# The attention phase of two layers, from four blocks one after the other to one stream of 80 slots

## The chip, the cores and the metric

The kernel is one program on one core of a Trainium2 chip. The metric is the time of one execution in microseconds on the device. The engines are TensorE (PE, with its weight loads as PEld), VectorE (DVE), ScalarE (ACT), GpSimd (POOL) and SyncE (SP, which only issues transfers here). They run in parallel, each through its own list of instructions in order, and wait for each other on semaphores.

## What is computed

An input of 512 positions by 1024 channels goes through two blocks of a network with three kinds of attention, and then through one block with dilated attention and a convolution. The change touches the attention of the first two layers, between the projections and the merging of the three branches:

```python
# 1: stick-breaking, 4 heads, weights from a cumulative sum over keys
w = exp(log_sigmoid(z) + tail);  o_a = w @ v
# 2: NSA, 8 heads in 2 groups, three parts, each with its gate
o_b = g0 * (softmax(q kc, compressed keys) @ vc) \
    + g1 * (softmax(q ks) @ vs) + g2 * (softmax(q kw) @ vw)
# 3: DSA, 4 heads over the 256 keys with the highest index score
score = sum_h(relu(iq_h @ ik) * iw_h)
o_c = softmax(q k[top 256]) @ v
merged = g_a * (o_a @ w_br_a) + g_b * (o_b @ w_br_b) + g_c * (o_c @ w_br_c)
```

All is float32. Where float32r is used, each factor is split in a high and a low part and three products are summed.

## The kernel before, in words

A layer is five phases: feed-forward, `mix1` (projections), `mix2` (attention), `mix3` (gates, branches, output), feed-forward. Between phases stands `fence`, at which all engines meet. The layers are one hardware loop of two rounds. The change is in `mix2`, whose four lists are `mix2_pe`, `mix2_act`, `mix2_dve` and `mix2_pool`, and in the order of the rows of one weight in the host's preparation.

`mix2` goes over four blocks `b` of 128 queries. Keys of block `b` are the first 128 (b + 1). A block has 20 jobs: batches 0 to 3 of four heads each are NSA (two for selected keys, two for the window), batch 4 is DSA. A job is: three score products (L893) into one of two banks; DVE adds the mask, turns the sign and takes the minimum (L1129); ACT takes the exponential and its sum `den` (L994) into `prob`. When a batch has its four jobs, DVE makes `coef`, one over the sum times the gate (L1112, L1117), ACT multiplies three heads of `prob` by it (L974) and POOL the fourth (L1035). PE then transposes the four heads for each key block (L905), ACT copies the result to `prob_t` (L1010), and PE multiplies it with the values (L915), 128 columns of values by 512 of weights, into the banks 4, 5 and 7. The columns of values are those of two groups, so half of each such result is not used. The compressed part is scaled in `cmp_p` and its product (L882) is summed in the same banks. At the end of a block ACT copies the used parts of the three banks to `o_t` (L1020).

The order is written by hand in slots. At slot `j` PE does the scores of job `j + 2`, then up to three `pieces` (transposes and value products of a batch that is complete), and then a step of `stick`, the stick-breaking attention of head `b`, whose products go to bank 6 (L818, L828, L830, L837) and whose exponentials and logarithm are at ACT's slots 7, 8 and 18. The slots run to 25 in each block. Before slot 0 of block `b` > 0 stand the eight index heads (L851, then ACT's relu L967 and DVE's sum L1078) and the compressed scores (L865, L1093 to L1106). For `b` > 0 DVE also picks the 256 highest index scores, eight in each of the jobs 0 to 15 (L1136, L1137), for the mask of batch 4.

At the start of `mix2`, ACT and DVE split the queries and keys into high and low parts, three tiles of 512 columns at a time (L979, L1083).

Of the kernel before, what the change touches and what calls it, by code (L numbers as in the profile page):

```python
# [7 lines left out]
P = 128  # L8
# [52 lines left out]
def program(nc, A, out, layers=L, dumps=()):  # L61
# [59 lines left out]
    relu, neg_s = val, sq  # L121
    index_s, picked, mask_k = ssq, val[0], val[1]
    prob = [part2.tensor(f"prob{i}", 4 * S) for i in range(2)]
    prob_t = [part2.tensor(f"prob_t{i}", S) for i in range(2)]
# [4 lines left out]
    kc_hi = idle.tensor("kc_hi", NC, F32R)  # L129
    assert idle.at <= w_hi_at + 8 * UNIT * 4  # L130
    cmp_s, cmp_t = (part2.tensor(n, 256) for n in ("cmp_s", "cmp_t"))
    cmp_p = cmp_s
    cmp_m = part2.tensor("cmp_m", 16)
    top8 = part2.tensor("top8", 8)
    neg_m = part2.tensor("neg_m", 80)
    den = part2.tensor("den", 80)
    coef = part2.tensor("coef", 80)
    zsq2 = relu
# [79 lines left out]
    for n in ("gains_in bias_tab_in bias_mm bias_out_a bias_out_v glu qk_out o_out conv job_parts mean centred c_norm c_val c_hi c_lo ya_out x_post y_norm "  # L218
              "sq_summed stat_sum stat_std stat_rs stat_diag rstd h_f32 h_hi h_lo "
              "dve_step x_val x_hi x_lo pad sb_out v_out t_out turned roped small_out hid cmp_mm cmp_turned mixer_in zn head_sum head_std gates vcb_zero "  # L220
              "job_red job_sc job_exp job_tr job_pv pt_out gate up gate_free rs_out hid_n hid_tr split_hi split_lo coef scaled_a scaled_p cmp_scaled sb_z sb_sp sb_c sb_w sb_o sb_d sb_zm sb_abs sb_e sb_ln idx_mm idx_relu idx_acc "
              "cmp_sc cmp_exp cmp_tr cmp_pt cmp_o cmp_sub merged_o o_hi o_lo o_tr sig branches part_sum m_val m_hi m_lo "
              "silu prod act_hi act_lo x_new sq zeroed ssq_add").split():
        s[n] = sem(n)
# [507 lines left out]
    def scores_q(tile_i, half, b):  # L732
        return heads_t[half, tile_i * S + b * P:tile_i * S + (b + 1) * P]

    JOBS, BATCHES = 20, 5
    ORDER = (0, 2, 1, 3)
    O_BANK = (4, 5, 4, 5, 7)  # L740

    def job(b, j):

        n, bt = (b + 1) * P, j // 4
        if bt < 4:
            c = ORDER[j % 4]
            half, t = slice(64 * (c // 2), 64 * (c // 2) + 64), 2 * (bt % 2) + c % 2
            key = (4 + bt // 2) * S
        else:
            c = j % 4  # L750
            half, t = slice(64 * (c % 2), 64 * (c % 2) + 64), 6 + c // 2
            key = 8 * S
        query = slice(t * S + b * P, t * S + (b + 1) * P)
        return bt, c, ((qk_hi[half, query], qk_lo[half, query]), (qk_hi[half, key:key + n], qk_lo[half, key:key + n]))

    def batch_values(bt, kb):

        if bt < 4:
            v0 = SB_H * HD + (bt // 2) * P
            return v_nat[:, kb * 512 + v0:kb * 512 + v0 + P]  # L760
        return small[:, kb * SMALL:kb * SMALL + P]

    def to_split():

        tiles = [slice(3 * i * S, 3 * (i + 1) * S) for i in range(3)]
        pairs = [(qk_hi[:, c], heads_t[:, c], qk_lo[:, c]) for c in tiles]
        return pairs[:2] + [(kc_hi[:], kc_t[:], kc_lo[:])] + pairs[2:]

    PASSES = ((0, 0), (0, 1), (1, 0))
# [4 lines left out]
    def score_bank(n):  # L774
        return bank[n % 2]

    SLOT_COUNT = JOBS + 5

    def pieces(b, j):


        bt, k = divmod(j - 6, 4)
        if not 0 <= bt < BATCHES or k > 2:
            return []
        seq = []
        for kb in range(b + 3):
            if kb <= b:
                seq.append(("turn", bt, kb))
            if kb >= 2:
                seq.append(("values", bt, kb - 2))  # L790
        if bt < 2:
            seq.append(("cmp", bt, 0))
        return seq[3 * k:3 * k + 3] if k < 2 else seq[6:]

    IDX_BANK = (2, 4, 5, 7)
    SB_OFF = {0: 0, 1: 512, 3: 896, 2: 1024}

    STICK_BLOCKS = ((0,), (1, 3), (2,))  # L800
    Z_MADE, Z_READ, SUM_MADE, SUM_READ = (0, 2, 4), (2, 4, 6), (11, 13, 15), (13, 15, 17)
    EXP_SLOT, LN_SLOT, SP_SLOT, W_SLOT, PV_SLOT, OUT_SLOT = 7, 8, 10, 18, 20, 22

    def mix2_pe(pe, f):
        fence(pe, f)
        def stick(h, slot):
# [34 lines left out]
        def index(b, heads):  # L841

            n = (b + 1) * P
            if 0 in heads:
                pe.wait_ge(s["o_out"], 3 * b)
                pe.wait_ge(s["pt_out"], turns_before(b, 0))
            for h in heads:
                if h >= 4:
                    pe.wait_ge(s["idx_relu"], 8 * (b - 1) + h - 3)
                rows = slice(32 * (h % 4), 32 * (h % 4) + 32)  # L850
                nc.tensor.matmul(bank[IDX_BANK[h % 4]][:, 0:n], heads_t[rows, (9 + h // 4) * S + b * P:(9 + h // 4) * S + (b + 1) * P],  # L851
                                 heads_t[rows, 11 * S:11 * S + n], start=True, stop=True).then_inc(s["idx_mm"], 1)

        def compressed(b):
            if b > 0:
                pe.wait_ge(s["idx_relu"], 8 * b)
            if b == 0:
                pe.wait_ge(s["split_lo"], 3)
            keys = (kc_hi[:], kc_lo[:])
            for h in range(4):  # L860
                query = slice(h * S + b * P, h * S + (b + 1) * P)
                for p, (qp, kp) in enumerate(PASSES):
                    for g in range(G):
                        half = slice(64 * g, 64 * g + 64)
                        mm = nc.tensor.matmul(bank[(2, 7)[g]][:, h * NC:(h + 1) * NC], (qk_hi, qk_lo)[qp][half, query], keys[kp][half, :],  # L865
                                              start=(p == 0), stop=(p == 2))
            mm.then_inc(s["cmp_sc"], 1)

        def compressed_turn(b):
            pe.wait_ge(s["cmp_scaled"], b + 1)  # L870
            for g in range(G):
                mm = nc.tensor.transpose(bank[7][:, g * P:(g + 1) * P], cmp_p[:, g * P:(g + 1) * P], ident)
            mm.then_inc(s["cmp_tr"], 1)

        def compressed_values(b, bt):

            pe.wait_ge(s["cmp_pt"], b + 1)
            probs = cmp_t[:].rearrange("p (g q) -> p g q", g=G)
            for i in range(2):
                h = 2 * bt + i  # L880
                dst = bank[O_BANK[bt]][:].rearrange("p (g i q) -> p g i q", g=G, i=2)[:, :, i, :]
                mm = nc.tensor.matmul(dst, vc_blk[:, h * P:(h + 1) * P], probs, start=False, stop=False)  # L882
            mm.then_inc(s["cmp_o"], 1)

        def scores(b, j):
            n = JOBS * b + j
            if n >= 2:
                pe.wait_ge(s["job_red"], n - 1)
# [1128 lines left out]
```

## Time and profile before

| | |
|---|---|
| three runs | 3994.3, 3997.73 and 4004.18 us, median 3997.73 |
| the profiled execution | 3993.57 us, its span 3992.0 us |
| mean granted clock of TensorE | 0.935 |
| busy in the span | PE 94%, PEld 75%, DVE 49%, ACT 40%, POOL 4% |

The span is the time from the first to the last instruction in the profile. The page divides it into 40 slices of about 100 us each. `mix2` lies from 572.9 to 872.2 us in the first layer and from 2002.6 to 2301.9 us in the second. A granted clock of 1.00 is TensorE's 2.4 GHz level and 0.50 its 1.2 GHz level; a number between them is a mean over a stretch.

### The profile page before, as it was taken

What the parts mean: (1) busy time and instruction counts of PE and PEld (TensorE: products, weight loads), DVE (VectorE), ACT (ScalarE), POOL (GpSimd) and SP (SyncE); (2) the same over time, 40 slices, a digit from 0 to 9 for tenths busy, and PEclk for the clock granted to TensorE, in tenths of its full rate; (3) what the DMA queues carried; (4) which work ended last, traced back from release to release, by engine and by line L of the source; (5) the groups of instructions that cost most, each with busy time, mean ns of one, the idle gap of its engine ahead of it and who ended that gap; (6) DMA issues with size and microseconds to landing.
All of it is one profiled execution on the core that took longest, in us unless ns stands there. A gap on an engine that the chain in (4) does not pass through costs nothing.

```text
span 3992.0 us, 47468 instructions
## 1 busy us (share of the span) xinstructions
PE 3745.1 (94%) x16932; PEld 2974.8 (75%) x16932; DVE 1942.5 (49%) x3241; ACT 1577.4 (40%) x2325; POOL 164.6 (4%) x157
## 2 busy tenths in 40 slices
PE   8999977789999999999868899999999998999998
PEld 6888764458888888888744478888887876878886
DVE  4443454555544434433645555444359773434443
ACT  4432345554343334422455544443232332424431
POOL 0000000000000000000000000000000001000001
PEclk9999977789999999999967799999999996998999
DMA  3233320002222323233210032223332210222231
GB/s 127 97 99 103 104 98 1 1 32 94 98 92 97 103 90 102 98 102 112 91 40 1 0 100 95 95 95 100 100 109 91 68 63 16 95 79 74 95 104 68
DMA packets 89160, 322.29 MB, mean 81 GB/s; under 512 B 10639, under 2 KB 10895, under 8 KB 89032
## 3 DMA queue, kind: packets, MB, share of 16 engines
q1 hardware_dynamic: 84384, 304.35, 23.0%
q0 software_dynamic: 3840, 13.17, 0.9%
q10 hardware_dynamic: 808, 3.07, 0.2%
q8 instruction: 78, 1.28, 0.1%
q14 instruction: 50, 0.41, 0.0%
HBM read 318.40 MB, written 10.02 MB: 82 GB/s over the span
## 4 chain that ended last, share of the span: by engine, by line
PE 48%; PEld 31%; issue 9%; DVE 6%; ACT 5%; PEldq 1%; POOLq 0%; DMA 0%; ACTq 0%; POOL 0%; DVEq 0%
PE bank L255 12%; PE bank L257 11%; PE bank L256 11%; PEld bank L257 10%; PEld bank L255 10%; PEld bank L256 10%; PE bank L915 2%; PE bank L1324 2%; PE bank L1351 1%; PE bank L905 1%; PE bank L893 1%; PE bank L1340 1%; DVE val L1478 1%; ACT prob_t L1010 1%; DVE sq L1129 1%
## 5 line engine op out<-in xcount | busy, mean ns | idle before, releaser
L251 DVE TENSOR_TENSOR unit_lo<-unit_raw,unit_hi 128x1024 fp32r<-128x1024 f32 x572 | 700.9, 1228 | 860.7 <-ACT unit_hi L246 851.7
L255 PE MATMUL bank<-h_hi,unit_hi 128*128 128x512 f32 x2688 | 1065.7, 396 | 26.3 <-DVE unit_lo L251 17.0
L257 PE MATMUL bank<-h_hi,unit_lo 128*128 128x512 f32 x2688 | 1056.0, 393 | 0.0
L256 PE MATMUL bank<-h_lo,unit_hi 128*128 128x512 f32 x2688 | 1055.6, 393 | 0.0
L246 ACT ACTIVATE unit_hi<-unit_raw 128x1024 fp32r<-128x1024 f32 x572 | 600.9, 1052 | 392.1 <-PE bank L257 381.6
L255 PEld LDWEIGHTS bank<-h_hi,unit_hi 128*128 128x128 f32 x2688 | 510.9, 190 | 139.6 <-DVE unit_lo L251 19.2
L257 PEld LDWEIGHTS bank<-h_hi,unit_lo 128*128 128x128 f32 x2688 | 510.4, 190 | 108.6
L256 PEld LDWEIGHTS bank<-h_lo,unit_hi 128*128 128x128 f32 x2688 | 511.3, 190 | 106.5 <-issue 1.7
L255 PE MATMUL bank<-act_hi,unit_hi 128*128 128x512 f32 x880 | 346.7, 394 | 0.0
L257 PE MATMUL bank<-act_hi,unit_lo 128*128 128x512 f32 x880 | 345.0, 392 | 0.0
L256 PE MATMUL bank<-act_lo,unit_hi 128*128 128x512 f32 x880 | 341.5, 388 | 0.0
L380 ACT ACTIVATE act_hi<-val 128x512 f32 x110 | 69.6, 632 | 467.6 <-DVE val L421 467.6
L257 PEld LDWEIGHTS bank<-act_hi,unit_lo 128*128 128x128 f32 x880 | 165.2, 188 | 38.7
L256 PEld LDWEIGHTS bank<-act_lo,unit_hi 128*128 128x128 f32 x880 | 165.2, 188 | 37.0
L255 PEld LDWEIGHTS bank<-act_hi,unit_hi 128*128 128x128 f32 x880 | 165.4, 188 | 32.9
L1478 DVE SCALAR_TENSOR_TENSOR val<-u_conv,block_columns,val 128x512 f32<-128x512 f32 x232 | 174.2, 751 | 7.2
L460 POOL TENSOR_TENSOR ssq<-ssq,sq 128x512 f32<-128x512 f32 x64 | 84.1, 1314 | 2199.9 <-ACT sq L392 1746.6
L255 PE MATMUL bank<-unit_hi,h_hi 128*128 128x512 f32 (+1 forms) x416 | 161.8, 389 | 10.7 <-ACT heads_t L571 10.7
L257 PE MATMUL bank<-unit_hi,h_lo 128*128 128x512 f32 (+1 forms) x416 | 160.5, 386 | 0.0
L256 PE MATMUL bank<-unit_lo,h_hi 128*128 128x512 f32 (+1 forms) x416 | 160.2, 385 | 0.0
L377 ACT ACTIVATE silu<-silu 128x512 f32<-128x512 f32 x110 | 69.5, 632 | 226.0 <-DVE silu L415 226.0
L419 DVE TENSOR_TENSOR val<-silu,bank 128x512 f32<-128x512 f32 x110 | 75.6, 687 | 160.8 <-PE bank L257 160.8
(272 smaller groups left out, 4501.0 us busy)
## 6 DMA issues: line engine op xcount, KB each, us to landing
unit_raw<-in_units SPq DMA_DIRECT2D x572, 512.0 KB, 3.3
bias_rows<-bias_once POOLq DMA_DIRECT2D x2, 3840.0 KB, 16.4
bias_t<-bias_rows POOLq DMA_DIRECT2D x16, 256.0 KB, 3.3
x<-in_x SPq DMA_DIRECT2D x4, 512.0 KB, 7.8
out_x<-x SPq DMA_DIRECT2D x8, 256.0 KB, 2.1
mixer_gains<-in_mixer_gains ACTq DMA_DIRECT2D x2, 736.0 KB, 5.1
mixer_constants<-in_mixer_constants ACTq DMA_DIRECT2D x2, 560.0 KB, 3.8
bias_t<-bias_rows POOLq DMA_DIRECT2D x8, 128.0 KB, 2.3
```

The source lines that it names most:

```text
L246: nc.scalar.activation(w_hi[u % SLOTS][:], raw[u % SLOTS][:], ACT.Copy).then_inc(unit_hi, 1)
L251: nc.vector.tensor_tensor(w_lo[u % SLOTS][:], raw[u % SLOTS][:], w_hi[u % SLOTS][:].bitcast(F32), ALU.subtract).then_inc(unit_lo, 1)
L255: nc.tensor.matmul(out_ap, w_h, r_h, start=first, stop=False)
L256: nc.tensor.matmul(out_ap, w_h, r_l, start=False, stop=False)
L257: return nc.tensor.matmul(out_ap, w_l, r_h, start=False, stop=last)
L377: nc.scalar.activation(silu[t][:], silu[t][:], ACT.Silu).then_inc(s["silu"], 1)
L380: nc.scalar.activation(act_hi[:, bass.ds(2 * i * S + t * S, S)], val[t][:], ACT.Copy).then_inc(s["act_hi"], 1)
L419: nc.vector.tensor_tensor(val[t][:], silu[t][:], bank[2 + t][:], ALU.mult).then_inc(s["up"], 1)
L460: nc.gpsimd.tensor_tensor(ssq[:], ssq[:], sq[m % 2][:], ALU.add).then_inc(s["ssq_add"], 1)
L915: nc.tensor.matmul(bank[O_BANK[bt]][:], batch_values(bt, kb), prob_t[products[0] % 2][:], start=(kb == 0 and bt in (0, 1, 4)), stop=(kb == ...
L1324: mm = nc.tensor.matmul(bank[2 + g][:, 0:w], t[half, q0 + b * P:q0 + (b + 1) * P], t[half, k0 + first_key:k0 + first_key + w], start=True, ...
L1478: ins = nc.vector.scalar_tensor_tensor(out=dst, in0=u_conv[:, u0 + k:u0 + k + S], scalar=w, in1=val[0][:], op0=ALU.mult, op1=ALU.add)
```

## The change

The four blocks become one stream of slots `q` from 0 to 87. Job `q` is block `q // 20`, job `q % 20`. At slot `q` PE does the scores of job `q` (no longer two ahead), the value product of the key block that was transposed two slots before, one transpose of four heads (`tile_of`), and the rest of the slot's work; ACT does the exponential of job `q - 1`. Batches, index heads and compressed steps of one block lie beside jobs of the next.

- The exponentials are no longer scaled. `coef` is spread over the partitions by small products (`spread_weights`: a column of `coef`, broadcast to 64 columns, times the identity), ACT copies that to `spread_c`, and DVE multiplies the 128x512 result with it (`merge_out`). For NSA it goes to `part_o`, and POOL adds it to `o_t`; for DSA it goes to `o_t` at once.
- A value product becomes two, each with the 64 value columns of one group and the 256 columns of weights that belong to it, one on partitions 0 to 63 of the result and one on 64 to 127. The results of two batches share a bank.
- The compressed result is evacuated by itself; its products are in 64-column halves too.
- Banks 2, 3 and 4 are a ring for all that ACT evacuates; results are in 5 and 7.
- Index heads come two in a slot, in slots 14 to 17 of the block before; `relu` and `picked` no longer share a buffer, `prob_t` has three buffers.
- The splits at the start are by one tile each, the first keys first.

```diff
-    SLOT_COUNT = JOBS + 5
+    Z_MADE, Z_READ, SUM_MADE, SUM_READ = (0, 2, 4), (1, 3, 5), (10, 12, 14), (11, 13, 15)
+    EXP_SLOT, LN_SLOT, SP_SLOT, W_SLOT, PV_SLOT, OUT_SLOT = 6, 7, 9, 16, 17, 19
+    LAG = 2
+    def tile_of(q):
+        n, kb = divmod(q - 5, 4)
+        return (n, kb) if 0 <= n < BATCHES * TB and kb <= n // BATCHES else None
+    def index_heads(q):
+        b, i = divmod(q - 14, JOBS)
+        return [(b + 1, 2 * i + e) for e in range(2)] if 0 <= b < TB - 1 and 0 <= i < 4 else []
+    def last_batch(b, k):
+        return BATCHES * b + (1, 3, 4)[k]
+    def weighted(q):
+        return next((g for g in GROUPS if q == 4 * last_batch(*g) + 5), None)
+    def spread(q):
+        return weighted(q - 1)
+    def merged(q):
+        return next((g for g in GROUPS if q == 4 * last_batch(*g) + 5 + g[0] + LAG + 1), None)
+    CMP_SCORES, CMP_SHIFT, CMP_EXP, CMP_SCALE, CMP_TURN, CMP_OUT = 2, 4, 6, 8, 10, 12
+    def ring_bank(use):
+        return bank[2 + ring_no[use] % 3]
...
+        def values(n, kb):
...
+            for h in range(2):
+                rows = slice(64 * h, 64 * h + 64)
...
+                mm = nc.tensor.matmul(dst[rows, cols], v, probs, start=(kb == 0 and bt in (0, 2, 4)), stop=(kb == b), skip_group_check=True)
+            mm.then_inc(s["job_pv"], 1)
+        def spread_weights(b, k):
+            pe.wait_ge(s["coef"], group_no(b, k) + 1)
+            dst = ring(("spread", b, k))
+            for i in range(4 if k < 2 else 2):
+                for h in range(2):
+                    m = place(b, 2 * k + i // 2, i % 2 + 2 * h) if k < 2 else place(b, 4, 2 * i + h)
+                    mm = nc.tensor.matmul(dst[64 * h:64 * h + 64, i * P:(i + 1) * P], coef[:, m:m + 1].to_broadcast([P, HD]), ident,
+                                          start=True, stop=True, skip_group_check=True)
+            mm.then_inc(s["ring_in"], 1)
...
+        for q in range(SLOT_END + 1):
+            b, at = divmod(q, JOBS)
+            if q < SLOTS2:
+                scores(q)
+            if tile_of(q - LAG):
+                values(*tile_of(q - LAG))
+            if tile_of(q):
+                turn(*tile_of(q))
+            for bh in index_heads(q):
+                index(*bh)
...
+            if spread(q):
+                spread_weights(*spread(q))
+            if b < TB:
+                stick(b, at)
...
-        def scale_probs(b, bt):
-            act.wait_ge(s["coef"], BATCHES * b + bt + 1)
-            for c in range(3):
-                head = prob[bt % 2][:, c * S:c * S + (b + 1) * P]
-                a = nc.scalar.activation(head, head, ACT.Copy, scale=coef[:, place(b, bt, c):place(b, bt, c) + 1])
-            a.then_inc(s["scaled_a"], 1)
...
+            for ib, h in index_heads(q):
+                m = 8 * (ib - 1) + h
+                src = arrives(("index", ib, h))
+                if m >= 2:
+                    act.wait_ge(s["idx_acc"], m - 1)
+                nc.scalar.activation(relu[m % 2][:, 0:(ib + 1) * P], src[:, 0:(ib + 1) * P], ACT.Relu).then_inc(s["ring_out"], 1)
...
-                nc.gpsimd.tensor_scalar(tile3, tile3, coef[:, place(b, bt, 3):place(b, bt, 4)], None, ALU.mult).then_inc(s["scaled_p"], 1)
+                nc.gpsimd.tensor_tensor(block_of(2, 4, b), block_of(2, 4, b), part_o[:].rearrange("p (i t) -> p i t", i=4),
+                                        ALU.add).then_inc(s["merged_o"], 1)
...
+        def merge_out(b, k):
+            g = group_no(b, k)
+            dve.wait_ge(s["job_pv"], tile_no(last_batch(b, k), b) + 1)
+            dve.wait_ge(s["ring_out"], ring_no["spread", b, k] + 1)
+            if k < 2:
+                p = 2 * b + k
+                if p >= 1:
+                    dve.wait_ge(s["merged_o"], p)
+                nc.vector.tensor_tensor(part_o[:], o_bank_of(b, k)[:], spread_c[g % 2][:], ALU.mult).then_inc(s["o_part"], 1)
...
-    heads_c = a["w_br_c"][l].reshape(2, 2, HD, D).transpose(1, 0, 2, 3).reshape(256, D)
-    branches = whole_units(np.concatenate([a["w_br_a"][l], heads_b, heads_c], 0))[None]
+    branches = whole_units(np.concatenate([a["w_br_a"][l], heads_b, a["w_br_c"][l]], 0))[None]
```

## Rows read from the trace of the kernel before

**Rows 1.** The page: span, busy time, granted clock in 40 slices, two groups.

```profile
span 3992.0 us, 47468 instructions
PE 3745.1 (94%) x16932; PEld 2974.8 (75%) x16932; DVE 1942.5 (49%) x3241; ACT 1577.4 (40%) x2325; POOL 164.6 (4%) x157
...
PEclk9999977789999999999967799999999996998999
...
L460 POOL TENSOR_TENSOR ssq<-ssq,sq 128x512 f32<-128x512 f32 x64 | 84.1, 1314 | 2199.9 <-ACT sq L392 1746.6
...
L419 DVE TENSOR_TENSOR val<-silu,bank 128x512 f32<-128x512 f32 x110 | 75.6, 687 | 160.8 <-PE bank L257 160.8
```

**Rows 2.** Busy time in the two windows of `mix2`: stretch, length, engines, clock, DMA.

```profile
572.90:872.20 299.30, 228.49 (x868) 139.67 (x868) 149.54 (x455) 165.59 (x360) 22.86 (x21) 0.75 0.04 14
2002.60:2301.90 299.30, 232.03 (x869) 141.86 (x870) 148.76 (x456) 164.23 (x360) 22.23 (x21) 0.73 0.03 13
```

**Rows 3.** Who waited for whom, first layer: us in total, times, longest.

```profile
ACT prob L994 <- DVE neg_m L1129: 49.4, 32, 4.8
...
PEld bank L893 <- DVE neg_m L1129: 25.3, 20, 3.6
...
PEld bank L905 <- ACT prob L974: 20.9, 9, 5.2
```

**Rows 4.** Timeline of PE at a block border: start, us, instruction, idle before.

```profile
696.25 0.93 PE L851 MATMUL bank<-heads_t 32*128 32x384 f32 x8 [2.44 <-ACT o_t L1020]
```

**Rows 5.** Busy time by 10 us in the last block, columns as in Rows 2.

```profile
790.00:800.00 10.00, 6.25 (x13) 3.06 (x14) 9.18 (x26) 3.15 (x8) 0.00 (x0) 0.50 0.00 1
800.00:810.00 10.00, 8.87 (x24) 5.77 (x23) 9.69 (x28) 5.08 (x12) 1.56 (x1) 0.50 0.00 0
...
830.00:840.00 10.00, 10.00 (x27) 5.44 (x27) 6.36 (x16) 6.06 (x13) 1.57 (x1) 0.76 0.01 2
840.00:850.00 10.00, 9.66 (x45) 6.10 (x44) 4.39 (x13) 3.00 (x7) 0.11 (x1) 1.00 0.00 0
```

**Rows 6.** Groups by line, first layer's window: count, busy us, mean ns.

```profile
L974 ACT ACTIVATE prob<-prob,coef 128x128 f32<-128x128 f32 (+3 forms) x60 | 29.1, 547 | 0.7 <-DVE coef L1112 0.7
L1010 ACT ACTIVATE prob_t<-bank 128x512 f32<-128x512 f32 x50 | 28.9, 596 | 47.4 <-PE bank L905 24.7 <-PE bank L915 22.4
...
L1020 ACT ACTIVATE o_t<-bank 64x256 f32<-64x256 f32 x24 | 9.1, 378 | 4.0 <-PE bank L915 3.7
```

**Rows 7.** The chain that ended last, in order of time: start, us, what.

```profile
635.86 2.76 PE bank L865 x24
...
682.10 0.55 PE bank L893 x3
...
846.05 0.89 PE bank L893 x3
...
848.43 0.86 PE bank L915 x2
...
853.63 0.60 PE bank L905 x4
...
860.70 2.16 PE bank L837 x8
```

**Rows 8.** Timeline of PE, two products of one score job.

```profile
843.43 0.39 PE L893 MATMUL bank<-qk_lo,qk_hi 64*128 64x512 f32 x1
843.65 0.39 PE L893 MATMUL bank<-qk_hi,qk_lo 64*128 64x512 f32 x1
```

**Rows 9.** Timeline of PE, the phase's first product.

```profile
579.09 0.40 PE L865 MATMUL bank<-kc_hi,qk_hi 64*128 64x32 f32 x2 [6.25 <-DVE kc_lo L1083]
```

**Rows 10.** Timeline of ACT, then of PE, around the table loads of the last block.

```profile
815.49 1.26 ACT L947 ACTIVATE sb_a<-sb_z 128x1280 f32<-128x1280 f32 x1
...
822.74 0.72 ACT L994 ACTIVATE prob<-sq,neg_m 128x512 f32<-128x512 f32 x1
...
825.45 2.98 PE L905 MATMUL bank<-constants,prob 128*128 128x128 f32 x12 [4.79 <-ACT prob L974]
```

More of the change, by code:

```diff
@@ L120, in program @@
     sb_a = part2.tensor("sb_a", 1280)
-    relu, neg_s = val, sq
-    index_s, picked, mask_k = ssq, val[0], val[1]
+    relu, neg_s, index_s = val, sq, ssq
     prob = [part2.tensor(f"prob{i}", 4 * S) for i in range(2)]
-    prob_t = [part2.tensor(f"prob_t{i}", S) for i in range(2)]
+    prob_t = [part2.tensor(f"prob_t{i}", S) for i in range(3)]
     idle = Place(nc, w_hi_at)
@@ L745, in job @@
+    Z_MADE, Z_READ, SUM_MADE, SUM_READ = (0, 2, 4), (1, 3, 5), (10, 12, 14), (11, 13, 15)
+    EXP_SLOT, LN_SLOT, SP_SLOT, W_SLOT, PV_SLOT, OUT_SLOT = 6, 7, 9, 16, 17, 19
+    def job(a):
+        b, j = divmod(a, JOBS)
+        bt = j // 4
         if bt < 4:
             c = ORDER[j % 4]
-            half, t = slice(64 * (c // 2), 64 * (c // 2) + 64), 2 * (bt % 2) + c % 2
-            key = (4 + bt // 2) * S
+            t, key = 2 * (bt % 2) + c % 2, 4 + bt // 2
+            half, need = slice(64 * (c // 2), 64 * (c // 2) + 64), 6 if bt >= 2 else t + 2
@@ L763, in to_split @@
[L763 to L769, printed above, removed]
+            t, key, half, need = 6 + c // 2, 8, slice(64 * (c % 2), 64 * (c % 2) + 64), 9
+        return b, bt, c, half, slice(t * S + b * P, t * S + (b + 1) * P), key * S, need
     def place(b, bt, c=0):
         return JOBS * b + 4 * bt + c
-    def score_bank(n):
-        return bank[n % 2]
@@ new lines, in ring_uses @@
+    def ring_uses(q):
+        b, at = divmod(q, JOBS)
+        uses = [("turn", *tile_of(q))] if tile_of(q) else []
+        uses += [("index", *bh) for bh in index_heads(q)]
+        if b < TB and at == CMP_SCORES:
+            uses += [("compressed", b, g) for g in range(G)]
+        if b < TB and at == CMP_TURN:
+            uses += [("turned", b, 0)]
+        if b < TB and at == CMP_OUT:
+            uses += [("compressed out", b, 0)]
+        if spread(q):
+            uses += [("spread", *spread(q))]
+        return uses
@@ L839, in stick @@
                 mm.then_inc(s["sb_o"], 1)
[L841 to L883, printed above, removed]
@@ new lines, in mix2_dve @@
+        for i, t in enumerate(QK_ORDER):
+            dve.wait_ge(s["split_hi"], i + 1)
+            nc.vector.tensor_tensor(tile(qk_lo, t), tile(heads_t, t), tile(qk_hi, t).bitcast(F32), ALU.subtract).then_inc(s["split_lo"], 1)
+        dve.wait_ge(s["split_hi"], 10)
+        nc.vector.tensor_tensor(kc_lo[:], kc_t[:], kc_hi[:].bitcast(F32), ALU.subtract).then_inc(s["split_lo"], 1)
+        for q in range(SLOT_END + 1):
+            b, at = divmod(q, JOBS)
+            if q < SLOTS2:
+                reduce(q)
+            for bh in index_heads(q - 1):
+                index_sum(*bh)
+            if weighted(q):
+                weigh(*weighted(q))
+            if merged(q):
+                merge_out(*merged(q))
+            if b < TB and at == CMP_SHIFT:
+                compressed_shift(b)
+            if b < TB and at == CMP_SCALE:
+                compressed_scale(b)
+            if b < TB:
+                stick(b, at)
```

402 lines of the change are left out of this document (198 added, 204 removed).

## The prediction

> **What bounds the kernel now.** I read the page first. TensorE (PE) is busy 94% of a span of 3992.0 us, and the slices of the granted clock (PEclk) show two places where that is lower: from slice 6 on and from slice 20 on, 7 tenths and less where it is 9 elsewhere [rows 1]. The windows of these places, from the phase fence before `mix2` to the one after, say that the attention phase takes 299.3 us in each of the two layers, 598.6 us together, that no engine fills it (PE 228 us, ACT 166, DVE 150, POOL 23), and that its mean granted clock is 0.75 and 0.73 [rows 2]. Outside it nothing is touched but the order of some weight rows. So the question is what 299.3 us becomes, twice.
>
> The chain of waits of the phase tells why no engine fills it. PE idles for score banks that DVE has not reduced (25.3 us at its weight loads), for the scaled exponentials of L974 (20.9); ACT idles for DVE's maxima (49.4) [rows 3]. Much of that is at the borders of the four query blocks: the next block's index heads start after the last copy of `o_t` (PE idle 2.44 us) [rows 4], and in the last block, from 790 to 810, DVE is at 9.2 and 9.7 of 10 us with scores and picks while PE has nothing to transpose yet and its clock is at 0.50 [rows 5]. From 840 to 850, with the pipeline full, the clock is 1.00.
>
> **Part by part.** All PE prices are at the 2.4 GHz level (clock 1.00).
>
> Removed: 60 scalings on ACT (29.1 us), 20 on POOL, 24 copies of `o_t` on ACT (9.1 us) [rows 6]. Added: 12 evacuations of spread weights and 4 of compressed outputs, each at most the 0.60 of a 128x512 copy like L1010, 8 small copies of compressed scores at about 0.3, so 12 us. ACT goes from 166 to about 140 us. DVE gets 8 products of 128x512 at about 0.69 (L419, one PSUM and one SBUF operand [rows 1]) and 4 half ones, less some small ones: 150 becomes about 156. Neither is the bound as a sum. POOL gets 8 additions of 128x512; the page has 1314 ns for such a one [rows 1]. They are hidden: the next merge that waits for one comes at least 4 slots later, and a slot is over 1 us; were that cover gone, they would cost 10 us in a layer.
>
> PE, for one layer: 20 score jobs of each block at 0.55 us for 256 keys and 0.89 for 512, so by that slope 0.38 and 0.72 for 128 and 384: 50.8. 50 transposes of four heads at 0.60: 30.0. 50 value products of 128x512 at 0.86: 43.0. Stick-breaking attention: four times 1280 columns for each head, 2.16 us each by L837: 34.6 [rows 7]. 1280 columns in 2.16 us is 1.69 ns a column. Spread weights are new: 20 products of 128 columns a block, 0.216 each, so 4.3 a block, 17.3 in all; this price is the change's own cost. Compressed branch: 24 products in 2.76 us at the 1.2 level, about 1.4 at the other, its values 8 x 0.216, two transposes 0.3: 13.6 in all [rows 7]. Index heads: four of 384 columns took 0.93 us together [rows 4], where 4 x 384 x 1.69 ns would be 2.6, so heads in different row quarters overlap; in pairs I take 0.61, 0.93 and 1.24 a pair, 12 pairs, 11.1. Sum 200.4 us.
>
> More switches between array shapes. A score job of 512 keys takes 0.89 in the chain, where its three products, by the 0.22 between the starts of two of them, take 0.66 [rows 7, 8]; the rest, 0.12 for a switch in and 0.12 for one out, is what I take a switch to cost. A slot had two (64-row scores, full array); now values use 64 columns, which makes three: 66 more, 8 us. PE: 208 us if the two 64-column halves run one after the other.
>
> The Trainium skill (TensorEngine Tiling (Array Packing), Tiling Modes) says that changing the tiling mode drains TensorE. That speaks against this change, and by this rule the price would be that of the rows, since the 0.12 us holds what a drain costs here.
>
> Do the halves overlap? The trace has no product on column halves. From above: not at all, since each half streams 256 columns and two of them are the 512 of before, 0.86. From below: fully, 0.43, as the four index heads did on row quarters [rows 4]. I take 0.43, as the nearest row is of a partial array with disjoint parts. It halves values, spread and compressed values: (43.0 + 17.3 + 6.9) / 2 = 33.6 less, so 175 us, still above DVE's 156. The Trainium skill (TensorE: Matmul & The Clock Gate, Part 3) gives three column tiles a measured speedup of 2.38; no run so far shows it here.
>
> The order. Jobs now run on through the block borders, two score banks deep as before; the turns and values of a block's last batches lie under the next block's first scores. So the border gaps go, and the phase is PE's own work plus:
> - Ends: from the fence to the first score. Splits in ninths rather than thirds let it start after two of the small splits, about 3.5 us after the fence instead of 6.2 [rows 9]; the last merge and the fence about 4.5. Together 8.
> - The table loads. In each block `stick` puts Abs, Exp, a table load, Ln and a second table load ahead of exponentials on ACT, 7.2 us from 815.49 to 822.74, in which ACT did one exponential; PE stood idle 4.79 [rows 10]. It stays: on ACT's queue behind it stand the exponentials and `prob_t`, and PE and DVE wait for these. I take 5 a block, 20; from below 8 (three slots of PE work stand in the queue), from above 28.
> - The clock. The phase starts at 0.50, and after the stall of the last block it is 0.76 from 830 to 840 [rows 5], with products at twice their price until about 834. PE work of 7 us in such a stretch costs 7 more. About 10 at the start and 5 a block: 30. From below 15, if it does not fall in the stalls.
> - Handshakes. New waits stand in the queues: DVE's merge waits for values and spread copies with the next reductions behind it, and ACT's relu of an index head waits for DVE's sum two heads before, with exponentials behind it. In those 12 slots a relu (0.60) and a sum (0.75) can be serial to the slot: 0 to 16 us. I take 10.
>
> Sum: 175 + 8 + 20 + 30 + 10 = 243 us. 299.3 - 243 = 56.3 us a layer, 112.6 in two. The profiled execution took 3993.57 us (its span and 1.6 around it, which stay); less 112.6 this is 3881. The median of the runs is 3997.73, 4.2 above, so 3885.
>
> **The rivals.**
> 1. The halves do not overlap: 208 + 68 = 276 us, 23 a layer, time 3951. For it: no row shows column halves overlapping. Against: the row quarters.
> 2. The stream hides more: table stalls 8 and clock 15, 216 us, 83 a layer: 3831. For it: between 840 and 850 PE worked nearly without a break at 1.00. Against: the same ACT chain is left.
> 3. Slower: the clock. The stream has few long gaps but many short ones, and from 800 to 810 PE was busy 8.87 of 10 us at 0.50 [rows 5]. If the whole stream stayed there with halves overlapping, PE would need 350 us, the phase 350 + 38 (the other terms) = 388, and the time 4175. It decides from a mean clock c where 175/c + 38 = 299.3, c = 0.67; with serial halves 208/c, c = 0.80. Against it: at 0.50 PE is the bound of each slot and has no gap, and after 10.00 busy of 10 us, from 830 to 840, the clock was up.
> 4. It doesn't do what it says: the border gaps only move into the slots. With serial halves 0.29 us more of waiting in each of 80 slots is enough, (299.3 - 276) / 80, and the time is within 12 us of 3998. For it: ACT's long wait for maxima, 49.4 us in 32 waits, is such waiting now [rows 3].
>
> **How the numbers follow.** Forecast (halves overlap, 3885, own range 3855 to 3920) 0.50; rival 1 0.25; rival 2 0.12; rival 4 0.05; rival 3 0.08. 0.3% of this kernel's time, 12 us, is about what a measurement can tell from no change. Faster than that: 0.50 + 0.25 + 0.12 = 0.87, within 0.05, slower 0.08. The range is 3831 to 3961: from rival 2's time to rival 1's 3951 with 5 us more of handshakes in each layer; outside are rivals 3 and 4 and half of 2.
>
> **What would show it.** The window between the same fences should be about 243 us in both layers. A value product's four instructions of 256 columns should start so that a pair takes 0.43 and not 0.86 at clock 1.00; the spread 0.85 for eight, not 1.7. No idle before the index heads. L974 and POOL's scalings gone, ACT near 140 us, DVE near 156. PE's longest waits should be for ACT after its table loads, four a layer. The mean clock should be above 0.85. The prediction is wrong if the clock stays under 0.7, if PE waits at merges or relus in each slot, or if halves are serial.

## The result, and the profile after

The changed kernel takes 3864.24 us (median of four runs, 3863.9 to 3875.02) against 4000.78 us for the kernel before beside it: ratio 0.9673, 95% interval 0.9654 to 0.9692. A second comparison gave 3863.73 against 3986.62 us, 0.9692 (0.9671 to 0.9712). I had forecast a gain of 112.6 us. It is 136.5 us between the first two medians, 122.9 in the second comparison, where the kernel before was quicker, and 129.2 between the two profiled executions (3993.57 and 3864.4 us).

The page after: span, busy time by engine, and the granted clock in 40 slices, beside [rows 1]:

```profile
span 3862.8 us, 48690 instructions
...
PE 3694.2 (96%) x17516; PEld 2948.0 (76%) x17516; DVE 1947.5 (50%) x3253; ACT 1520.3 (39%) x2217; POOL 141.2 (4%) x133
...
PEclk9999988899999999999879999999999987989999
```

The two phases, from ACT's copy of `kc_t` to `mix3`'s first split. The first view is of the kernel before, whose second phase [rows 2] had some 5 us too late; the second is of the changed kernel. Columns: stretch, length, busy us (count) of PE, PEld, DVE, ACT, POOL, granted clock, DMA share, GB/s.

```profile
572.88:872.21 299.33, 228.49 (x868) 139.67 (x868) 149.54 (x455) 165.61 (x360) 22.86 (x22) 0.75 0.04 14
1997.42:2299.02 301.60, 231.52 (x868) 141.36 (x868) 149.52 (x455) 165.61 (x360) 22.87 (x21) 0.73 0.04 14
```

```profile
561.71:797.93 236.22, 204.79 (x1160) 126.95 (x1160) 152.09 (x461) 137.19 (x307) 11.34 (x10) 0.84 0.05 18
1933.60:2170.08 236.48, 204.97 (x1160) 126.85 (x1160) 152.09 (x461) 137.20 (x307) 11.27 (x10) 0.84 0.05 18
```

The phases went from 600.9 to 472.7 us together, 128.2 less. The span is 129.2 shorter, so the gain is in the phases and nowhere else. PE is busy 25 us a layer less although it has new products; its idle time in the phase went from 70.5 us (300.5 less 230.0) to 31.5. ACT is at 137 us (forecast 140), DVE at 152 (156), the clock at 0.84 (I had asked for more than 0.85).

PE's lower busy time looks to be the clock's doing, and not less work. This is an estimate: I weighed its busy time by the granted clock in windows of 1 us, as if a microsecond at half clock did half of the work. By this estimate the first layer's phase holds 172 us of full-clock work before and 177 after, and the half clock adds 56 us before and 28 after. Two layers of a run below have the same products but 48 us more of busy time at half clock, and that cost 20.6 us; at this price it is 180 and 181 us of work, and 48 and 24 us for the clock. So of the 63 us that the phase lost 39 are idle time (70.8 to 31.4 us), and the 24 of busy time are, by this estimate, all the clock's. What the halves save must have gone into the new products and the change of shape in every slot; no run takes these apart but for the spread weights.

What PE waits for in the first phase now, in total, times, longest ([rows 3] has PEld's waits; PE's own wait for the scaled exponentials of L974 was 18.5 us):

```profile
PE bank L847 <- ACT prob L1012: 17.6, 5, 6.0
...
PE bank L838 <- DVE neg_m L1167: 4.3, 6, 1.9
...
PE bank L929 <- DVE sb_z L1089: 3.3, 4, 1.2
```

The first is the table loads' stall, now the largest wait left. Timeline of the first block: the two loads on ACT with the logarithm between them, then the transposes that had waited:

```profile
582.29 1.28 ACT L988 ACT_TABLE_LOAD   x1
...
583.58 1.36 ACT L988 ACTIVATE sb_a<-sb_a,constants 128x1280 f32<-128x1280 f32 x1
...
584.96 1.28 ACT L1012 ACT_TABLE_LOAD   x1
...
586.80 1.11 PE L847 MATMUL bank<-constants,prob 128*128 128x128 f32 x4 [5.97 <-ACT prob L1012]
```

The index heads, which stood idle 2.44 us before their first product [rows 4], start without a gap. Their group in the first phase: count, busy us, mean ns, idle before:

```profile
L884 PE MATMUL bank<-heads_t 32*128 32x256 f32 (+2 forms) x48 | 13.1, 533 | 0.1
```

Timeline of PE in the last block at full clock: a value product in 64-column halves (L867), four transposes (L847), eight spread products (L877), the next scores.

```profile
783.95 0.65 PE L867 MATMUL bank<-prob_t,v_nat 128*64 128x256 f32 x4
784.53 0.66 PE L847 MATMUL bank<-constants,prob 128*128 128x128 f32 x4
785.12 1.09 PE L877 MATMUL bank<-constants,coef 128*64 128x128 f32 x16
786.14 0.49 PE L838 MATMUL bank<-qk_hi 64*128 64x512 f32 x1
```

Read by starts, the value product holds PE for 0.58 us, a switch included, where the one of before took 0.86 [rows 7]; the transposes 0.59; the spread weights 1.02 for eight.

### The profile page after: what moved, and what is told of

Same layout as the page of the kernel before. It is cut to its first block, busy times and chain, and to the rows that moved or that the text cites. A ratio compares the mean times of both kernels' runs of the same rounds, so it can differ in the third digit from the quotient of the medians.

```text
span 3862.8 us, 48690 instructions
## 1 busy us (share of the span) xinstructions
PE 3694.2 (96%) x17516; PEld 2948.0 (76%) x17516; DVE 1947.5 (50%) x3253; ACT 1520.3 (39%) x2217; POOL 141.2 (4%) x133
## 4 chain that ended last, share of the span: by engine, by line
PE 49%; PEld 32%; issue 10%; DVE 5%; ACT 3%; PEldq 1%; POOLq 0%; DMA 0%; POOL 0%; DVEq 0%; ACTq 0%
PE bank L253 12%; PE bank L255 12%; PE bank L254 12%; PEld bank L255 11%; PEld bank L253 11%; PEld bank L254 10%; PE bank L1378 2%; PE bank L1405 2%; PE bank L847 1%; PE bank L867 1%; PE bank L1394 1%; DVE val L1532 1%; PE bank L838 1%; PE bank L877 1%; PE bank L939 1%
## 5 line engine op out<-in xcount | busy, mean ns | idle before, releaser
L244 ACT ACTIVATE unit_hi<-unit_raw 128x1024 fp32r<-128x1024 f32 x572 | 600.9, 1052 | 394.0 <-PE bank L255 380.4
L253 PEld LDWEIGHTS bank<-h_hi,unit_hi 128*128 128x128 f32 x2688 | 511.6, 190 | 134.8 <-DVE unit_lo L249 14.5
L253 PEld LDWEIGHTS bank<-act_hi,unit_hi 128*128 128x128 f32 x880 | 165.5, 188 | 32.8
```

What stands on the lines that cost most here:

```text
L244: nc.scalar.activation(w_hi[u % SLOTS][:], raw[u % SLOTS][:], ACT.Copy).then_inc(unit_hi, 1)
L253: nc.tensor.matmul(out_ap, w_h, r_h, start=first, stop=False)
```

## The experiments

The phases in the profiled execution (first and second layer, us), and the ratio to the kernel before:

| kernel | phases | clock | ratio (95%) |
|---|---|---|---|
| before | 299.3, 301.6 | 0.75, 0.73 | 1 |
| before, halves | 290.6, 290.9 | 0.70, 0.69 | 0.9966 (0.9950 to 0.9981) |
| before, unscaled | 289.0, 291.7 | 0.75, 0.74 | 0.9953 (0.9939 to 0.9967) |
| before, both | 276.3, 277.1 | 0.70, 0.72 | 0.9903 (0.9873 to 0.9933) |
| changed | 236.2, 236.5 | 0.84, 0.84 | 0.9673 (0.9654 to 0.9692) |
| changed, again | 236.1, 236.6 | 0.84, 0.84 | 0.9692 (0.9671 to 0.9712) |
| values on the whole array | 255.4, 246.3 | 0.82, 0.86 | 0.9757 (0.9729 to 0.9784) |
| no logarithm | 225.7, 225.4 | 0.85, 0.85 | 0.9625 (0.9598 to 0.9652) |
| dummies in the stall | 228.0, 228.8 | 0.90, 0.88 | 0.9685 (0.9669 to 0.9701) |
| spread twice | 256.2, 256.4 | 0.78, 0.78 | 0.9787 (0.9759 to 0.9816) |
| logarithm later | 224.6, 237.5 | 0.84, 0.75 | 0.9651 (0.9635 to 0.9667) |
| later, direct | 219.2, 220.6 | 0.84, 0.84 | 0.9648 (0.9628 to 0.9669) |
| later, dummies | 227.8, 235.7 | 0.89, 0.86 | 0.9668 (0.9647 to 0.9689) |
| later, direct, dummies | 233.6, 226.9 | 0.86, 0.89 | 0.9652 (0.9631 to 0.9672) |

**Whether the halves run together.** One part undone in the changed kernel:

```diff
-                rows = slice(64 * h, 64 * h + 64)
+                rows = slice(0, P)
...
-                    v, cols, probs = v_nat[:, v0:v0 + HD], ...
+                    v, cols, probs = v_nat[:, v0:v0 + P], ...
```

> The changed kernel, with its 50 value products a layer on the whole array again: 128 value columns, the same 256 moving columns, two instructions into the same bank region (so what they add to the bank is the sum over both halves and not the two halves apart; sizes and order of the other work are kept). Spread weights and compressed values stay on halves. Theory (the two 64-column halves run together, and TensorE's work is most of each slot): a value product goes from 0.58 back to about 0.86 and one switch of array shape less a slot gives 0.12 back, so 0.16 to 0.28 more in 50 products, 8 to 14 us a layer, the phase 244 to 250 instead of 236.3, the ratio to the kernel before 0.971 to 0.975. Rival (halves are serial, or the slots are set by DVE and ACT so that TensorE's time is free): phase 230 to 237, ratio 0.964 to 0.968.

The phases are 19.2 and 9.8 us longer, 14.5 on average, the first at a clock of 0.82 and the second at 0.86. PE at full clock in this run, a value product, the transposes, the next scores:

```profile
764.78 1.13 PE L867 MATMUL bank<-prob_t,small 128*128 128x256 f32 x4
765.75 0.60 PE L847 MATMUL bank<-constants,prob 128*128 128x128 f32 x4
766.28 0.50 PE L838 MATMUL bank<-qk_hi 64*128 64x512 f32 x1
```

By starts it is 0.97 us against 0.58. So the halves run together: 0.39 us a product, 19.5 us for 50 at full clock, of which 14.5 arrived. The rival of serial halves is out. My expectation held 0.58, which has a switch in it, against 0.86, which has none, so even its high end of 0.28 was too small; the first layer's phase and the ratio lie above its ranges.

**The parts alone, in the kernel before.** Halves for its value products:

```diff
-            nc.tensor.matmul(bank[O_BANK[bt]][:], batch_values(bt, kb), prob_t[products[0] % 2][:], ...
+            for h in range(2):
+                mm = nc.tensor.matmul(bank[O_BANK[bt]][64 * h:64 * h + 64, 256 * h:256 * h + 256],
+                                      batch_values(bt, kb)[:, 64 * h:64 * h + 64],
+                                      prob_t[products[0] % 2][:, 256 * h:256 * h + 256], ...
```

> The kernel before with one part of the change alone: value products (and the compressed branch's values) as two 64-column halves of 256 moving columns each. Theory that the halves overlap and count: 80 value products less the scale of 0.28 each, and one switch more, 0.12: 50 x 0.16 to 0.28 = 8 to 14 us a layer at the most; as much of the phase's time in this kernel is gaps and waits for ACT, I take half, 4 to 10 us a layer, ratio 0.995 to 0.998. Rival, that halves pay only where slots are full: no change, 0.999 to 1.001, or slower by the switches, up to 6 us a layer, 1.003.

No scaling:

```diff
-            pe.wait_ge(s["scaled_a"], BATCHES * b + bt + 1)
-            pe.wait_ge(s["scaled_p"], BATCHES * b + bt + 1)
+            pe.wait_ge(s["job_exp"], JOBS * b + 4 * bt + 4)
...
-                    scale_probs(b, j // 4 - 1)
```

> The kernel before with the scaling of the exponentials left out (ACT's 60 at L974 and GpSimd's 20; the transposes wait for the exponentials alone, so the outputs are not normalised or gated). Theory: PE's waits for the scaled tiles, 20.9 us a layer, and ACT's 29.1 us of work go, and half of that shows, 10 to 20 us a layer, ratio 0.990 to 0.995. Rival (the streaming is the whole gain; DVE's maxima set the slots anyhow): under 4 us a layer, 0.998 to 1.000.

And the two together:

> The kernel before with both: values on column halves and no scaling of the exponentials (outputs not normalised or gated). What is left between this and the changed kernel is the stream of slots across block borders with its new work (spread weights, merges). Theory that the parts add: 14 to 30 us a layer, phase about 278, ratio 0.985 to 0.993; then the stream is worth 35 to 50 us a layer, most of the 65. Rival (each part frees what the other needs, so that together they give more than the sum): phase under 265, ratio under 0.983, and the stream is worth less than half of the gain.

Halves alone give 9.7 us a layer, no scaling 10.1, both 23.8, a little more than the sum; no interval of the three ratios holds 1. These are the theories' sizes, only the ratio without scaling is just over its range of 0.990 to 0.995. Of the 64.1 us a layer that the change gives, the stream of slots with its new products is therefore worth 40.3, and it has to pay for the spread weights first. In the first layer 36.1 of this is idle time (67.6 to 31.4 us) and 4.0 is PE's busy time, at a clock of 0.84 where it was 0.70. The 40.3 is a difference between two kernels: no run takes the stream apart (the block borders, the earlier first score, the ring of banks, the clock).

In the kernel before, the halves cut PE's busy time by 15.7 us in the first layer's phase. By the estimate above that is 22 us less work and 6 us more for the half clock (0.75 became 0.70), and 7.0 us more of waiting took the phase's gain down to 8.8. The halves' gain looks larger in the stream (14.5 on average), but one of its two layers has 9.8, so this is not shown. So all three parts count; the stream is the largest.

**The table loads' stall.** In the changed kernel the logarithm (L988) becomes an Abs:

```diff
-                nc.scalar.activation(sb_a[:], sb_a[:], ACT.Ln, bias=one_col).then_inc(s["sb_ln"], 1)
+                nc.scalar.activation(sb_a[:], sb_a[:], ACT.Abs, bias=one_col).then_inc(s["sb_ln"], 1)
```

> The changed kernel with the natural logarithm of the stick-breaking branch replaced by Abs, an operation of the table already loaded (that branch's output is then not the reference's); the two table loads a block, 2 x 1.28 us, go, and no other work. Theory: the four waits of TensorE for the exponentials (6.0, 4.0, 3.2 and 4.0 us) are the table loads' doing as to 2.6 us each, 10 us a layer, and the low clock behind them comes from these waits, so that another 5 to 10 us a layer go: phase 216 to 221. Rival A: only the loads' own time, phase 224 to 227. Rival B: the waits are set by DVE, which is as busy there (3.8 of 4 us), phase 232 to 236.

The phases are 10.5 and 11.1 us shorter, for 8 loads of 1.28 us, 10.3: rival A. PE's wait for the exponentials, first layer:

```profile
PE bank L847 <- ACT prob L1012: 6.3, 5, 3.1
```

17.6 became 6.3. PE's busy time did not move (204.9 against 204.8), nor did the clock (0.85 against 0.84). That shorter stalls alone bring the clock back is refuted.

**Dummy products in the stall.** Four a block, ahead of the transposes of slot 9:

```diff
+            if b < TB and at == 9:
+                pe.wait_ge(s["sb_zm"], 3 * (b + 1))
+                for i in range(4):
+                    nc.tensor.matmul(bank[6][:], ones, mask_c, start=True, stop=True)
             if tile_of(q):
                 turn(*tile_of(q))
```

> The changed kernel with four dummy products of 128x512 more in each block, written to the free bank 6 just ahead of the transposes of slot 9, where TensorE waits for the exponentials behind the table loads (nothing reads them). At full clock they are 3.4 us, which the waits of 3.2 to 6.0 us hold; at half clock 6.9 us, which they don't. Theory that the low clock behind a stall comes from TensorE's idle time in it: in the last block, where the clock falls in the stall, it stays up, and the phase loses up to 5 us there; in the blocks where it is down before the stall the dummies cost 3 us each: phase 233 to 242. Rival (idle time is not what lowers it, or what was idle before counts): the clock falls where it did, every block pays 3 us, phase 245 to 248.

Ten us around the stall of the last block, the changed kernel first, then this one:

```profile
750.00:760.00 10.00, 7.51 (x34) 5.01 (x35) 7.70 (x20) 6.10 (x13) 0.00 (x0) 0.55 0.00 0
```

```profile
750.00:760.00 10.00, 9.45 (x49) 4.86 (x46) 9.03 (x25) 8.96 (x16) 0.00 (x0) 1.00 0.00 0
```

The clock stays up there, and the phases are 8.2 and 7.7 us shorter although PE has 19.4 us of dummies more in the first; that is even under the range I gave the theory. PE's idle time took in 15.9 us of them (31.4 became 15.6), and its other work took 11.7 us less, at a clock of 0.90 and not 0.84. So what PE does in the stall does bear on the clock behind it. Yet the runs are no faster: 3865.31 against 3864.24 us, ratios 0.9685 and 0.9673. In the profiled execution 15.9 us less in the phases meet 10 more in `mix1`, by the clock as told below: 3858.5 against 3864.4 us. The other three runs took 3863.51 to 3868.22 us, with a mean clock of 0.954 to 0.955 over the program where the profiled one had 0.958; they have no profile, so where they lost that stays open.

**The spread weights' own cost.** Issued twice:

```diff
-            for i in range(4 if k < 2 else 2):
+            for i in 2 * tuple(range(4 if k < 2 else 2)):
```

> The changed kernel with the products that spread the weights issued twice into the same columns of the bank (same results): what they cost on the path. Busy they are 1.09 us for eight in a full-clock stretch, 1.98 at half clock, about 12 us a layer in all; my forecast had 8.7 us. Theory (TensorE's work is what each of these slots takes): phase longer by 8 to 12 us, ratio to the kernel before 0.971 to 0.974. Rival (they lie under the other engines' time): under 3 us a layer, ratio 0.967 to 0.969.

The phases are 20.0 and 19.9 us longer, more than either theory. The group of the spread products, first the changed kernel's, then this one's:

```profile
L877 PE MATMUL bank<-constants,coef 128*64 128x128 f32 x160 | 14.9, 339 | 0.1
```

```profile
L877 PE MATMUL bank<-constants,coef 128*64 128x128 f32 x320 | 27.7, 342 | 0.1
```

They take 12.8 us more; the other 11.5 of the 24.3 us by which PE's busy time grows are other products, at a mean clock of 0.78 where it was 0.84. Windows of the last block, before the clock fell, at half clock, and where it rose:

```profile
730.00:754.00 24.00, 23.96 (x160) 14.24 (x161) 17.40 (x45) 14.63 (x34) 1.27 (x1) 0.99 0.01 1
754.00:786.00 32.00, 32.00 (x106) 17.27 (x104) 23.78 (x61) 17.10 (x31) 1.27 (x1) 0.50 0.00 1
786.00:790.00 4.00, 4.00 (x33) 3.09 (x30) 0.00 (x0) 1.30 (x3) 0.00 (x0) 0.77 0.00 0
```

The clock fell with PE at work in 23.96 of the 24 us before, stayed at half for 32 us in which PE had no gap, and rose again without one.

**The logarithm a slot later.** Same work, other order on ACT:

```diff
-    Z_MADE, Z_READ, SUM_MADE, SUM_READ = (0, 2, 4), (1, 3, 5), (10, 12, 14), (11, 13, 15)
-    EXP_SLOT, LN_SLOT, SP_SLOT, W_SLOT, PV_SLOT, OUT_SLOT = 6, 7, 9, 16, 17, 19
+    Z_MADE, Z_READ, SUM_MADE, SUM_READ = (0, 2, 4), (1, 3, 5), (11, 13, 15), (12, 14, 16)
+    EXP_SLOT, LN_SLOT, SP_SLOT, W_SLOT, PV_SLOT, OUT_SLOT = 6, 8, 9, 17, 18, 19
```

> The changed kernel with the logarithm one slot later on ACT (its end of slot 8 instead of slot 7), and what follows it in stick-breaking one slot later too; no work is added or removed. TensorE's transposes of slot 9 wait for the exponential of ACT's slot 8, which then stands ahead of the two table loads and not behind. Theory (order of ACT's queue makes the waits of 17 us a layer): a good half of it goes, phase 222 to 229, ratio 0.960 to 0.964. Rival (the next score bank or sum waits for the same logarithm a slot later, and the wait only moves): phase 234 to 238.

In the first layer PE's wait for the exponentials is almost gone, and little took its place:

```profile
PE bank L877 <- DVE coef L1140: 2.3, 2, 2.1
PE bank L847 <- ACT prob L1012: 2.3, 2, 1.9
PE bank L877 <- ACT prob_t L1019: 2.2, 2, 1.2
```

The phase is 11.6 us shorter. The second layer runs the same instructions in 237.5 us. Its row, beside the first's:

```profile
572.80:797.44 224.64, 203.69 (x1160) 127.19 (x1160) 151.87 (x461) 135.58 (x306) 11.32 (x9) 0.84 0.05 19
1922.00:2159.49 237.49, 224.24 (x1160) 138.21 (x1160) 152.19 (x461) 135.93 (x307) 11.31 (x10) 0.75 0.05 18
```

PE's idle time is 13.3 us there, less than the 21.0 of the first, and PE is busy 20.6 us longer on the same 1160 products: the difference is the clock. The wait went in both layers (2.3 us is left of it in each); what was won in the second was lost to the clock. The longest of the second layer's stretches at half clock, and what stood ahead of it, have no gap of PE either:

```profile
2074.00:2091.00 17.00, 17.00 (x112) 10.30 (x110) 11.70 (x30) 11.00 (x27) 0.27 (x1) 0.99 0.01 2
2091.00:2125.00 34.00, 34.00 (x112) 18.19 (x111) 24.74 (x64) 18.24 (x33) 1.00 (x1) 0.50 0.00 0
```

The ratio, 0.9651, is just above the theory's 0.964.

**Combinations.** The changed kernel again:

> The changed kernel as it is, once more, beside the next three. Outside the two phases the profiled executions so far took either about 3390 or about 3400 us, as a stretch of 24 us at half clock stood in the projections ahead of one of the two phases or of both. Expected: the same phases, 236.2 and 236.5, and a ratio of 0.965 to 0.970; if the clock's stretches are chance from run to run, phases that differ by up to 10 us from these.

The phases agree with the first run within 0.2 us; one of its five runs was some 9 us over the others (3872.99). The logarithm taken directly:

```diff
-                nc.scalar.activation(sb_a[:], sb_z[:], ACT.Abs).then_inc(s["sb_abs"], 1)
-                act.wait_ge(s["sb_abs"], h + 1)
-                nc.scalar.activation(sb_a[:], sb_a[:], ACT.Exp, scale=-1.0).then_inc(s["sb_e"], 1)
+                nc.scalar.activation(sb_a[:], sb_z[:], ACT.Exp).then_inc(s["sb_e"], 1)
...
-                nc.vector.scalar_tensor_tensor(out=sb_a[:], in0=sb_z[:], scalar=0.0, in1=sb_a[:], op0=ALU.max,
-                                               op1=ALU.add).then_inc(s["sb_sp"], 1)
```

> The logarithm a slot later, and ln(1 + exp(z)) taken directly: ACT's Abs (1.27 us a block) and DVE's maximum and sum of 128x1280 (1.48 us a block) go. The same value where exp(z) does not overflow, so it holds for these inputs and not for all. Theory (ACT's burst and DVE's load in the first half of a block set what TensorE waits for): 4 to 8 us a layer below the version with the logarithm later alone, whose first layer took 224.6: phase 217 to 221, ratio 0.960 to 0.963. Rival (TensorE's own work and clock are now the bound): phase 222 to 226 where the clock is alike, ratio 0.964 to 0.966.

Phases as the theory has them, 219.2 and 220.6. In one comparison on one chip it took 3845.35 us and the changed kernel 3863.73, 18.4 less; the phases of the profiled execution, its fastest (3830.14), are 32.8 less, so the other runs must have lost some of it again. Their mean clock over the program was 0.946 to 0.951 and that of the profiled one 0.955. Then dummies, one in each of slots 7 to 9 and two in slot 10:

```diff
+    KEEP = {7: 1, 8: 1, 9: 1, 10: 2}
...
+            if b < TB and at in KEEP:
+                pe.wait_ge(s["sb_zm"], 3 * (b + 1))
+                for i in range(KEEP[at]):
+                    nc.tensor.matmul(bank[6][:], ones, mask_c, start=True, stop=True)
```

> The logarithm a slot later and five dummy products of 128x512 a block in slots 7 to 10, 4.3 us of TensorE at full clock, where DVE and ACT set the pace. The version without dummies had 75 us at half clock in the first layer's phase and 120 us in the second's (224.6 and 237.5 us). Theory (dummy work in the waits keeps the clock up, which is worth more than it costs): both phases 220 to 227, mean clock over 0.87, ratio 0.960 to 0.964. Rival (with the waits gone the dummies stand in the way): phases 228 to 240, ratio 0.966 to 0.970.

> All three together: logarithm later, taken directly, and the five dummy products a block. If the two effects add, phase 214 to 221 and ratio 0.957 to 0.962; if TensorE is the bound once the burst is shorter, the dummies cost their 4.3 us a block in part, phase 222 to 230, ratio 0.963 to 0.967.

Both ratios went as the rival said, and three of the four phases about so; the fourth, 233.6 us, is above its 222 to 230. The clock rose, but with the stall gone the dummies have little cover: with the direct logarithm PE's busy time grows by 18.2 us in the first layer and its idle time falls by only 3.8. The two phases grow by 20.7 us together, and the medians from 3845.35 to 3850.81. Of the versions that hold for all inputs, the logarithm a slot later is the fastest measured: 3852.84 us, all four runs within 1.3 us. It was not run beside the changed kernel, and the ratios' intervals (0.9635 to 0.9667, 0.9654 to 0.9692) overlap, so that it is faster is likely and not shown; its first-layer phase shows the mechanism.

## Why the prediction was right

The forecast, halves overlapping in a stream and 3885 us, was the case that came, 20.8 us above the measured median. By its own terms, first layer:

- **PE's work and the half clock.** 175 and 30, 205 together; PE was busy 204.8 us. The halves (0.43 and a switch of 0.12, 0.55) took 0.58; whole-array values in the same stream took 0.97, the 0.86 of before and one switch, 0.11. The Trainium skill (TensorEngine Tiling (Array Packing), Theoretical Speedup) promises up to 2x for a dimension of 64; with the switch in, the rows show 0.97 / 0.58 = 1.7. Eight spread products took 1.02, not 0.85, as the change of shape counts there too. I take these 0.17 us and the 0.15 by which 0.58 is over half of 0.86 to be switches; no run has one alone. By the estimate under the result the 205 are 177 to 181 us of work and 24 to 28 for the half clock. The clock fell where I had it, "about 10 at the start and 5 a block": PE's 20.4 us of work at half clock at the start cost 10, and behind that 3.0 and 13.0, 10.6 and 8.2 us cost 8, 5 and 4.

```profile
561.71:593.70 31.99, 20.37 (x98) 14.09 (x99) 14.65 (x52) 20.32 (x46) 1.14 (x1) 0.50 0.32 124
607.70:610.70 3.00, 3.00 (x5) 1.36 (x5) 0.00 (x0) 1.48 (x6) 0.00 (x0) 0.50 0.00 0
624.70:641.70 17.00, 13.00 (x54) 8.67 (x55) 12.29 (x45) 12.67 (x23) 0.00 (x0) 0.50 0.01 1
682.70:696.70 14.00, 10.58 (x44) 6.75 (x45) 11.02 (x34) 10.77 (x18) 0.00 (x0) 0.51 0.00 0
750.70:760.70 10.00, 8.21 (x35) 5.20 (x36) 7.03 (x19) 6.12 (x13) 0.00 (x0) 0.51 0.00 0
```

- **The table loads.** 20; PE waited 17.6 for the exponentials, nearly all in one wait of 3.2 to 6.0 us a block. Without the loads 10.8 us a layer went; the rest is what else stood on ACT's queue.
- **Ends.** 8; it was 4.7. First score 3.1 us after the start (I had 3.5); from PE's last product to the end of the phase 1.6, not 4.5. The last merge is 0.42 us and the fence costs little: that term was mis-sized.
- **Handshakes.** 10. All idle time is 31.4 us (236.2 less 204.8); less 17.6 and 4.7 that leaves 9.1. The size came, the path that I named did not show: ACT's relus of index heads did wait for DVE's sums (6.0 us in all), but PE stood idle at none of them. Its waits were 4.3 us for DVE's maxima and 3.3 us for the stick-breaking scores.

The sum is 236.2 against 243: 2.4 too much for stalls, 3.3 for ends, 0.9 for handshakes, 0.2 for PE. The other 2.3 us of the 15.6 by which the phases gained more than forecast are the second layer's phase before, 301.6 and not 299.3.

Rival 1 (serial halves) is refuted by the whole-array run, rival 4 (gaps only move) by the idle time. Rival 2 named the right next lever, the table stalls: with the direct logarithm the phases came to 220 us. That this is near its 216 is in part luck, as its other term, a clock that costs 15 us, did not come: PE was busy 204.3 us as before. Rival 3 (the clock stays down) did not come either, and the clock gave 24 to 28 us of the first layer's gain. But my argument against it was wrong. I took it that an engine without gaps at 0.50 gets its clock back, from one row after a busy stretch [rows 5]; the windows with the spread weights issued twice show PE without a gap and at half clock for 32 us, and those with the logarithm later for 34. That the changed kernel's clock is 0.84 was the outcome, not something that my reasons secured.

## What to carry to other kernels

Look at what a stream of slots leaves uncovered, not at the share of an engine: here two thirds of the gain came from the stream, in which a block's work starts under the end of the last, and a third from cheaper products and less scaling. Count the busy time by its clock before calling it work: PE was busy 24 us less in the phase, and about as much as that was time at half clock. Products that use half of their columns should go to column halves when the other half of the array has independent work; count a switch of array shape (estimated here at 0.11 to 0.15 us) against them. A burst on an engine that others wait for costs by its place in the queue: putting the logarithm and its two loads behind the exponential that PE waited for, and not ahead of it, took 11.6 us from a phase of 236 where the clock was the same (0.84), and nothing in the other layer, where the clock fell to 0.75.

## What the runs showed of the hardware

**A busy TensorE can stay at half clock.** Besides the windows above, a stretch of 24 us in `mix1`, some 46 us ahead of the phase, stood at 0.50 in one layer or in both. First the changed kernel's two layers, then the same distances from the phase with the dummies in the stall:

```profile
515.70:539.70 24.00, 20.56 (x167) 18.79 (x166) 16.45 (x61) 10.43 (x23) 0.00 (x0) 1.00 0.25 88
1887.60:1911.60 24.00, 23.46 (x126) 23.14 (x128) 12.44 (x54) 6.25 (x15) 0.00 (x0) 0.50 0.14 45
```

```profile
522.10:546.10 24.00, 23.54 (x126) 23.21 (x128) 12.45 (x54) 6.25 (x15) 0.00 (x0) 0.50 0.13 45
1886.70:1910.70 24.00, 23.63 (x136) 23.31 (x138) 12.44 (x54) 6.67 (x14) 0.00 (x0) 0.52 0.13 45
```

In the kernel before:

```profile
527.60:551.60 24.00, 24.00 (x149) 23.67 (x149) 13.10 (x55) 5.89 (x13) 0.00 (x0) 0.50 0.13 45
1952.00:1976.00 24.00, 20.55 (x182) 18.85 (x183) 16.42 (x61) 10.62 (x22) 0.00 (x0) 1.00 0.27 88
```

In the changed kernel the stretch begins at a wait of PE of 2.70 us; the same wait in the other layer (10 us nearer to the phase, as what lies between goes faster) left the clock at 1.00:

```profile
526.43 0.34 PE L253 MATMUL bank<-unit_hi,h_hi 128*128 128x160 f32 x1 [2.70 <-ACT heads_t L569]
1888.14 0.50 PE L253 MATMUL bank<-unit_hi,h_hi 128*128 128x160 f32 x1 [2.70 <-ACT heads_t L569]
```

The spans less the phases show its price: 3391.1 us for the kernel before and 3390.1 for the changed one, each with one such stretch, and 3400.1 for the third, with both, so some 10 us, in code that no experiment touches. In the kernel before it stood in the first layer, in the changed one in the second; that moves 10 us from one layer to the other and changes no sum. It is likely a part of what separates runs of one kernel: the changed kernel's run of 3875.02 us had a mean clock of 0.949 over the program, the three of 3864 us 0.954. The Trainium skill (TensorE: Matmul & The Clock Gate, What's actually happening) says that the lower clock is the default and activity releases it. The dummies, which kept the clock up in the last block's stall, agree with it; these stretches, with PE busy 23.5 of 24 us at 0.50, and those of 32 and 34 us above, with no gap at all, do not. What decides there stays open. No experiment was made on `mix1`.
